# Last feed-forward stage with seven block products, and another order in the second block's mixers and first choice of experts

## What is computed

```
def swiglu(x, w_gu, w_down):                      # D_FF = 2816
    gate, up = jnp.split(x @ w_gu, 2, axis=-1)
    return (jax.nn.silu(gate) * up) @ w_down

def hybrid_layer(x, mem_n, ...):
    h = layer_norm(ALPHA * x + 0.5 * swiglu(x, ffn1...), ln_g[0], ln_b[0])
    ... merged = gated sum of the three branches ...
    h = layer_norm(ALPHA * h + merged @ w_out, ln_g[1], ln_b[1])
    return layer_norm(ALPHA * h + 0.5 * swiglu(h, ffn2...), ln_g[2], ln_b[2])

def second_block(x, mem, ...):
    for l in range(DEPTH):
        xn = rmsnorm(x, norm_mix[l]); proj = xn @ w_in[l]
        u_pool, u_conv, u_diff, u_sc, u_mem = jnp.split(proj, ...)
        cat = stack of pool_mixer, conformer_conv (31 taps), diff_attention, short_conv, memory_attention
        x = x + rmsnorm(cat, group_norm[l]) @ w_out[l]
        x = x + peer_ffn(rmsnorm(x, norm_ffn[l]), peer_wq[l], peer_subkeys[l], peer_u[l], peer_v[l])

def peer_ffn(xn, wq, subkeys, u_tab, v_tab):
    q = (xn @ wq).reshape(b, s, 8, 2, 128)
    top_s, top_i = lax.top_k(einsum(q, subkeys), 16)
    best, ci = lax.top_k(sums of the two halves' 16 x 16 scores, 16)
    idx = top_i[first, ci // 16] * 128 + top_i[second, ci % 16]
    g = softmax(best)
    out = sum over the 8 x 16 picks of g * gelu(u_tab[idx] . xn) * v_tab[idx]
```

## Time and profile before

| | us |
|---|---|
| median of 3 runs | 3241.88 (3241.27 to 3243.1) |
| the profiled execution | 3243.7 |
| its span | 3241.9 |
| TensorE busy in the span | 3016.5 (93%) |
| VectorE busy | 1940.5 (60%) |
| ScalarE busy | 644.6 (20%) |
| GpSimd busy | 615.3 (19%) |
| last feed-forward stage, gate-up from its second slab to the end of the way down | 1359 to 1581 |
| mixers and gathers, first layer | 1581 to 2414 |
| mixers and gathers, second layer | 2414 to 3235 |

### The profile page before, as it was taken

One profiled execution on the slowest core, in us unless ns is written; L12 is line 12 of the kernel. 1 busy time (PEld: TensorE's weight loads), 2 busy tenths in 40 slices (PEclk: granted clock), 3 DMA queues, 4 the chain that ended last, 5 costly groups with the idle time before them and its releaser, 6 DMA issues.

```text
span 3241.9 us, 34946 instructions
## 1 busy us (share of the span) xinstructions
PE 3016.5 (93%) x13098; PEld 2009.3 (62%) x13098; DVE 1940.5 (60%) x4473; ACT 644.6 (20%) x1581; POOL 615.3 (19%) x558
## 2 busy tenths in 40 slices
PE   8999999999999999999999888888989988888887
PEld 8958997995976898786685333333448643333322
DVE  7744432776764523210275877777757487777775
ACT  1113121111102223010153111111125321111110
POOL 0010000101001000100012434443421144444442
PEclk9999999999999999999999999999999999999999
DMA  6443223444543323464336999999983599999998
GB/s 232 174 157 128 104 92 129 178 174 156 195 171 141 130 79 115 145 248 154 112 116 237 422 421 418 417 412 414 420 357 119 202 421 421 421 412 416 416 417 351
DMA packets 114937, 830.38 MB, mean 256 GB/s; under 512 B 12880, under 2 KB 13136, under 8 KB 14160
## 3 DMA queue, kind: packets, MB, share of 16 engines
q0 software_dynamic: 73728, 536.90, 40.0%
q1 hardware_dynamic: 39456, 281.29, 24.1%
q10 hardware_dynamic: 1584, 9.95, 0.8%
HBM read 827.05 MB, written 1.05 MB: 255 GB/s over the span
## 4 chain that ended last, share of the span: by engine, by line
PE 65%; DMA 23%; DVE 6%; issue 4%; ACT 1%; POOL 0%; POOLq 0%; DVEq 0%; SPq 0%; ACTq 0%
DMA arena<-table_uv,idx 22%; PE bank L348 11%; PE bank L2444 9%; PE bank L443 9%; PE bank L503 6%; PE bank L701 5%; PE bank L375 4%; PE bank L430 4%; PE bank L937 3%; PE bank L2131 2%; PE bank L2316 2%; DVE arena L3025 1%; PE bank L599 1%; DVE diag L3033 1%; PE bank L2390 1%
## 5 line engine op out<-in xcount | busy, mean ns | idle before, releaser
L2444 PE MATMUL bank<-arena,diag 128*128 128x512 f32 x2048 | 1019.3, 624 | 187.7 <-DVE diag L3033 181.1
L2444 PEld LDWEIGHTS bank<-arena,diag 128*128 128x128 f32 x2048 | 361.5, 193 | 721.2 <-DVE diag L3033 453.3
L3025 DVE CUSTOM_DVE_ANT_0 arena<-arena 128x1024 f32<-128x1024 f32 x512 | 625.6, 1222 | 262.2 <-DMA arena<-table_uv,idx 258.9
L3109 POOL DMA_INDIRECT arena<-table_uv,idx x512 | 542.8, 1060 | 931.3 <-PE bank L2444 717.0
L2681 ACT ACTIVATE dots<-dots 128x1 f32<-128x1 f32 x512 | 103.8, 203 | 1089.9 <-DVE dots L3025 1089.6
L1811 POOL TENSOR_TENSOR x_tok<-arena,ktail 128x1024 f32<-128x1024 f32 (+1 forms) x12 | 27.0, 2251 | 1531.2 <-ACT arena L967 1531.2
L348 PE MATMUL bank<-x,ring 128*128 128x256 f32 x1440 | 316.0, 382 | 0.0
L348 PEld LDWEIGHTS bank<-x,ring 128*128 128x128 f32 x1440 | 275.5, 192 | 39.6 <-issue 1.9
L3033 DVE TENSOR_SCALAR diag<-cst,dots,soft 128x128 f32<-128x128 f32 x512 | 175.9, 344 | 0.0
L701 PE MATMUL bank<-x,ring 128*128 128x256 f32 x768 | 173.1, 379 | 0.0
L701 PEld LDWEIGHTS bank<-x,ring 128*128 128x128 f32 x768 | 143.2, 190 | 18.8 <-issue 1.0
(11 more groups left out here) (556 smaller groups left out, 4064.4 us busy)
## 6 DMA issues: line engine op xcount, KB each, us to landing
ring<-stream SPq DMA_DIRECT2D x258, 1024.0 KB, 4.8
arena<-table_uv,idx POOLq DMA_INDIRECT x512, 13.0
ktail<-ln_rows ACTq DMA_DIRECT2D x6, 1024.0 KB, 5.0
arena<-mem_rows SPq DMA_DIRECT2D x2, 1024.0 KB, 9.7
arena<-stream SPq DMA_DIRECT2D x2, 1024.0 KB, 6.9
sq<-keys ACTq DMA_DIRECT2D x2, 1024.0 KB, 4.7
cst<-consts SPq DMA_DIRECT2D x1, 1547.0 KB, 8.1
cst<-consts SPq DMA_DIRECT2D x1, 1089.0 KB, 14.4
```

The source lines that it names most:

```text
L2444: last = mm(bank[4 + 2 * tt + half][:, :], diag[:, n % DIAGS, :], row_slot(n)[:, D + 512 * half:D + 512 * half + 512], start=(h == 0 and k ...
L3025: v.tensor_tensor_reduce(u, u, tok[:, tt, :], 1.0, 0.0, ALU.mult, ALU.add, dots[:, tt, k:k + 1]).then_inc(u_used.sem, 1)
L3109: g.indirect_dma_start(out=row_slot(n), out_offset=None, in_=peer_uv, in_offset=bass.IndirectOffsetOnAxis(ap=idx[:, h % 2, tt, k:k + 1], a ...
```

## The change

The last feed-forward stage goes through `ffn_by_seven` too, and `ffn` is gone. Its sums have tiles of their own (`last_gu_space` of two sets instead of three, `last_down_space`, `last_x_space`, `last_h_space` with three sets, `last_r_space`, `last_p_space`), as the tiles of the other stages are overwritten by the second block's preparation. Hidden pairs are summed one at a time (`one_pair_sums`): pair 0 after slab 3, pair 1 after the last gate-up slab, the others ahead of the weight sums of the same slab on the way down. The norm is `norm_by_seven` with `last_rows` in place of the channel copies; before the second block TensorE waits for the first tile's scaling. SyncE loads memory rows and parameters with slabs 6 and 7 of the stage, and constants and the second block's first four slabs with slabs 25 to 29, ahead of the constants waiting for all hidden chunks. VectorE clears one tile a slab (slabs 5 to 9) and scales the memory rows at slab 11; the transposes of the memory go through two banks, one tile after slab 12 and one after slab 13.

In the mixers three roots of heads are taken as three Ln and three Exp; the copy of the pool projection stands after the fourth exponential; taps 8 to 10 of the convolution stand ahead of the difference and 11 to 20 behind it. The first choice of experts finds and writes eight numbers, then the other eight; gathers 0 to 7 need the first signal only, gather 8 the second.

```diff
+EARLY_AFTER = (6, 7) + tuple(range(GU_SLABS + 3, GU_SLABS + 8))
+EARLY_IN_GU = 2
...
+        last_gu_space = ((by_head(kT), by_head(qT)), (by_head(xaq), by_head(swq)))
+        last_down_space = ((by_tile(Q)[:, 0:HALF], by_tile(Q)[:, HALF:D], by_tile(qkT)[:, 0:HALF], flat_mem[:, 0:HALF]),
+                           tuple(arena[:, n * T:n * T + HALF] for n in (16, 18, 20, 22)),
+                           tuple(flat_x[:, n * HALF:n * HALF + HALF] for n in range(4)))
...
-                early = n - ((DEPTH - 1) * SLABS + FFN2_AT[DEPTH - 1] + 6)
-                if 0 <= early < EARLY_LOADS:
-                    if early == 0:
+                early = n - ((DEPTH - 1) * SLABS + FFN2_AT[DEPTH - 1])
+                if early in EARLY_AFTER:
+                    i = EARLY_AFTER.index(early)
+                    if i == 0:
                         sp.wait_ge(slab_done.sem, slab_done.at(DEPTH - 1, FFN2_AT[DEPTH - 1]))
-                    during_last(sp, early)
+                    if i == EARLY_IN_GU:
+                        sp.wait_ge(hid_ready.sem, hid_ready.at(DEPTH - 1, 2 * FC))
+                    during_last(sp, i)
...
-                to_channels(l, 2 * f, 0, y)
...
+                if last_stage(l, f):
+                    pe.wait_ge(z_dve.sem, z_dve.at(l, 2 * 2 + 1))
+                else:
+                    to_channels(l, 2 * f, 0, y)
...
+            def one_pair_sums(l, f, w):
+
+                dve.wait_ge(hid_ready.sem, hid_ready.at(l, f * FC + (2 if w == 0 else FC)))
+                if w >= 3:
+                    dve.wait_ge(slab_done.sem, slab_done.at(l, FFN2_AT[l] + GU_SLABS + w - 1))
+                a11, a12 = hidden[:, 2 * w, 0:P], hidden[:, 2 * w + 1, 0:P]
+                a21, a22 = hidden[:, 2 * w, P:T], hidden[:, 2 * w + 1, P:T]
+                s1, s2, s3, s4 = (hidden_sum((l, f), w, q) for q in range(1, 5))
+                step.did(v.tensor_tensor(s1, a21, a22, ALU.add))
+                step.did(v.tensor_tensor(s3, a11, a21, ALU.subtract))
+                dve.wait_ge(step.sem, step.n - 1)
+                step.did(v.tensor_tensor(s2, s1, a11, ALU.subtract))
+                step.join()
+                v.tensor_tensor(s4, a12, s2, ALU.subtract).then_inc(hs_ready.sem, 1)
...
-                    if j % 4 == 3 or j == GU_SLABS - 1:
+                    if last_stage(l, f):
+                        if j == 3:
+                            one_pair_sums(l, f, 0)
+                        during_last(dve, j)
+                    elif j % 4 == 3 or j == GU_SLABS - 1:
                         pair_sums(l, f, j // 4)
...
+                if last_stage(l, f):
+                    one_pair_sums(l, f, 1)
                 for i in range(GU_SLABS + 2, W_SLABS):
+                    if last_stage(l, f):
+                        one_pair_sums(l, f, i - GU_SLABS)
                     weight_sums(l, f, at, i)
...
-                by_channel(l, n, 0, x, gain, shift)
+                if final:
+                    last_rows(0)
+                else:
+                    by_channel(l, n, 0, x, gain, shift)
...
-                else:
-                    norm(l, 1, OUT_AT + OUT_SLABS)
-                    ffn(l, 1, FFN2_AT[l])
-                    norm(l, 2, SLABS)
+                norm(l, 1, OUT_AT + OUT_SLABS, lambda: weight_sums(l, 1, FFN2_AT[l], 0))
+                ffn_by_seven(l, 1, FFN2_AT[l])
+                norm_by_seven(l, 2, (lambda: weight_sums(l + 1, 0, FFN1_AT[l + 1], 0)) if l < DEPTH - 1 else None)
...
+            tt = j - MEM2_T_AT
+            if 0 <= tt < TT:
+                pe.wait_ge(mem_scaled, tt + 1)
+                if tt > 0:
+                    pe.wait_ge(mem_copied, 2 * tt)
...
+                def head_roots(*heads):
+                    for n, i, b in heads:
+                        act.wait_ge(qk_ms.sem, qk_ms.at(l, n + 1))
+                        step.did(fn(sq[:, 2 * i:2 * i + 2, :].rearrange("p c t -> p (c t)"), bank[b][:, :], ACT.Ln, bias=eps[:, 0:1]))
+                    step.join()
+                    for n, i, b in heads:
+                        root = sq[:, 2 * i:2 * i + 2, :].rearrange("p c t -> p (c t)")
+                        fn(root, root, ACT.Exp, scale=-0.5).then_inc(qk_std.sem, 1)
...
-                head_root(0, 1, 3)
-                head_root(1, 2, 4)
-                head_root(2, 0, 5)
+                head_roots((0, 1, 3), (1, 2, 4), (2, 0, 5))
...
+                    if n == POOL_COPY_AT:
+                        read(fn(pp[:, :, POOL_EDGE:POOL_EDGE + T], projected(S_POOL)[:, :].rearrange("p (a t) -> p a t", a=GT),
+                                ACT.Copy), S_POOL)
...
-                conv_part(8, 14)
+                conv_part(8, 11)
...
-                conv_part(14, 21)
+                conv_part(11, 21)
...
+                def first_choice():
+
+                    keys_first8(0, 0)
+                    keys_masked(0, 0)
+                    keys_next8(0, 0)
...
+                    step.did(v.max(best[:, 0, 0:8], sums))
+                    step.join()
+                    step.did(v.max_index(besti[:, 0:8], best[:, 0, 0:8], sums))
+                    places_of_half(0)
+                    step.did(v.match_replace(masked[:, :], best[:, 0, 0:8], sums, -3e38))
...
+                    v.max_index(besti[:, 8:16], best[:, 0, 8:16], masked[:, :]).then_inc(best_ready.sem, 1)
+                    dve.wait_ge(best_ready.sem, best_ready.at(l, 1))
+                    places_of_half(1)
...
-                for k in TOPK_PARTS:
-                    topk_part(0, 0, k)
+                first_choice()
...
-                        passed(idx_ready, idx_ready.at(l, h * TT + tt + 1))
+                        passed(idx_ready, idx_ready.at(l, 1 if n == 0 else h * TT + tt + 2))
+                    if n == TOPK // 2:
+                        passed(idx_ready, idx_ready.at(l, 2))
```

225 lines of the change are left out of this document (108 added, 117 removed).

## The result

The changed kernel takes 3222.91 us (median of 4 runs, 3222.45 to 3225.39); the kernel before, on the same chip, 3242.49. The ratio is 0.9938 with a 95% interval of [0.9926, 0.9949], so 16.5 to 24 us less. I had predicted 3219, range 3210 to 3228.

What follows compares the result with a forecast made beforehand. It took TensorE to bound the work from the last feed-forward stage into the second block, and DMA the gathers. Gains of 12.2 (stage), 9.6 (mixers) and 1.0 (first choice) sum to 22.8: 3241.9 to 3219 us, range 3210 to 3228.

Steps and rivals of the forecast that it cites:

- Steady part of the stage: Last feed-forward stage: 22 gate-up slabs take 133.3 us instead of 152, the last part 66.09 instead of 75.53.
- Entry: Start of the last feed-forward stage: VectorE's sums delay the x sums to about 1360.3; TensorE idles some 3.6 us.
- Handover: Last stage to second block: first tile ready 10.7 us after the last matmul; TensorE idles 3.8 us; transposes gain 15.2.
- rival (c): Clock doesn't fall at the two seams and gathers start 1.6 earlier at no price: 3212 to 3215, chance 0.13.
- two falls at 1.5 each: At the last stage's start and end, each new TensorE idle causes a clock fall costing 1.5 us, bounds 0 and 3.0.
- The stage's term, 12.2: Last feed-forward stage: net gain of 12.2 us, from 15.2 at the second block's transposes less 3.0 for clock falls.
- Mixers: Both layers' mixers: fewer table loads, earlier exponentials and moved taps gain 4.8 us a layer, 9.6 together.
- The eight steps beside GpSimd: Mixers: VectorE's steps to the difference overlap GpSimd's pool sums and lose 1.8 us, bounds no loss and 3.0.
- 3.0 from the Trainium skill: Mixers: upper bound of VectorE's loss before the difference, 3.0 us, if blocked by all GpSimd work left.
- One sign of being wrong: Mixers: a difference ready later than 16 us after the maxima would show the prediction wrong.
- First choice: First choice of experts: earlier gathers against a later second tile gain net 0.5 us a layer, bounds -0.5 and 1.6.
- the queue runs dry by 1.1 us: Gathers: ninth comes 1.2 us later, first eight end 1.6 earlier; with 1.7 us in hand the queue runs dry by 1.1.

Runs made afterwards that it cites:

- after_again: The changed kernel as it is, measured a second time beside the other runs: 3223.94 us, ratio 0.9943 to the kernel before.
- late_signal: The changed kernel, but GpSimd issues its first gather only when all sixteen numbers of the first choice are written: 3224.48 us.
- old_choice: The changed kernel with the first choice of experts and its signals as they were before: 3221.62 us.
- choice_fill: The changed kernel with 16 extra matmuls on TensorE where it stands still before the second tile's transposes: 3223.38 us.
- stage_alone: The kernel before with only the last feed-forward stage changed to seven products: 3230.59 us against 3243.6.
- mixers_alone: The kernel before with only the mixers changed (roots, pool copy, convolution taps): 3234.16 us against 3243.6.
- roots_alone: The kernel before with only three logarithms put before three exponentials for the head-square roots: 3239.63 us against 3243.6.
- choice_spread: The changed kernel, with the spread order: first eight numbers, second tile's sums, second eight maxima, their numbers during transposes; gate exponentials after the second tile's root: 3219.57 us.
- after: The changed kernel, all parts together, against the kernel before: 3222.91 us, ratio 0.9938.
- taps_back: The changed kernel with the convolution's taps split as before (8 to 13, then 14 to 20): 3226.79 us, ratio 0.9950 to the kernel before.

## Why the prediction was right, and where not

The measured 3222.9 is 4 us from the forecast of 3219. That it is not further off is partly luck, as two errors of opposite sign meet in the sum (end of this section).

- **Steady part of the stage**: right. From the x sums to the last part 135.9 us (forecast 136.0, with 0.61 of waiting at slab 12 for 0.9), the last part 66.1.
- **Entry**: right in its end in this profile, not in its parts. The x sums start at 1359.77 (forecast 1360.3), as the two slow weight sums cost the forecast 2.8 us each. TensorE's idle time is 1.99 for the third slab's fetch and 0.86, not 3.6 in one, and a fall of the clock between them (0.74 and 0.84 in the four us from 1352 and from 1356) fills the rest. VectorE ends this stretch, so the fall costs nothing: I had charged 1.5. How the four sums meet GpSimd's row operations differs between profiles: in four of the ten profiles with the new stage (after_again, late_signal, old_choice, choice_fill) only one of them was slow, and in the first three of these the x sums began 6.6 us after the start of VectorE's scaling instead of 8.7.
- **Handover**: right. TensorE waited 3.07 us (forecast 3.8), the clock fell to 0.57 for four us and the 16 value products took 1.2 us more there than for the second tile. But it doesn't fall each time: it did in five of the eight profiles that have this wait. In the profile of old_choice it stayed at 1.00 at both seams:

```profile
1350.00:1358.00 8.00, 5.92 (x49) 5.29 (x48) 7.33 (x14) 2.61 (x6) 5.84 (x2) 1.00 0.53 184
1566.00:1574.00 8.00, 4.94 (x27) 4.15 (x26) 5.75 (x11) 6.50 (x14) 2.98 (x2) 1.00 0.35 131
```

  That is rival (c) for the stage: the bet on two falls at 1.5 each was not safe. The stage's term, 12.2, measured 14.7 in the trace and 13.1 by stage_alone. Of the 2.5 more in the trace, 1.2 are the transposes' earlier start (16.4 ahead, not 15.2) and 1.3 the falls: 3.0 charged, 1.7 paid.
- **Mixers**: right, step by step. 9.6 forecast, 9.9 in the trace, 9.4 by mixers_alone. The wait before the scores is gone, the one at the difference 0.76 (forecast 0.8), the one at the convolution's mean 0.75 (1.0). The exponentials took 8.9 us with the copy (8.8), from their start to the difference 16.85 (16.8). By the Trainium skill (ScalarE: Activation LUTs, "Table sets: the hidden batching unit") Ln and Exp would have shared a table and 2.07 us a layer would have stayed. The trace shows a load of 1.28 us at each switch, and roots_alone the 4.0 us that went with them. The eight steps beside GpSimd cost 1.37 (4.62 against 3.25), for which the sum had 1.8. I had worked out 3.0 from the Trainium skill (SBUF — State Buffer, "Who interferes with whom"), by which two engines on the shared ports exclude each other for a whole instruction. In the four rows under **The taps** the trace agrees with that rule; what was wrong is my use of it, as if all that GpSimd had left stood in front of VectorE, while VectorE had begun first on one of the two long ones. One sign of being wrong was badly set: a difference later than 16 us after the maxima. It came 16.9 after them, and by my own times it would have come 16.9 after them too, so that sign tells nothing.
- **First choice: wrong, with the wrong sign by the bytes.** Forecast a gain of 0.5 a layer, bounds -0.5 and 1.6; by the bytes it is 1.5 behind at 60 us and 1.1 at 640, outside the bounds either way. The early start did come (7.87 against 10.06 us) and gained 1.0, as allowed. The ninth gather was forecast 1.2 later and came 2.6 and 1.9 later. What failed is the sentence that the queue runs dry by 1.1 us. I had let the ninth gather be late by VectorE's 1.2 alone. I had written myself that TensorE stands still in front of these transposes and that its clock falls there, and did not see that behind a longer standstill the fall is longer (about 3 or 7 us behind 2.95, about 7 or 10 behind 4.35). The second tile was 1.4 late, TensorE's first use 2.3 in the mean, and the eighth gather, which needs the second tile's queries to have left its slot, was 3.5 and 1.3 late (24.8 and 24.1 us after the score copy, before 21.3 and 22.8); I had left it out. So the loss by 60 us was 2.5, not 1.1.

In the trace the three add up to 14.7 + 9.9 - 4.2 = 20.4, against 12.2 + 9.6 + 1.0 = 22.8: the stage and the mixers gave 2.8 more than forecast, the choice 5.2 less (1.1 to 1.5 of its 2.1 a layer by the bytes, 1.4 by the means over five profiles each, the rest within the gathers' varying rate). So half of the choice's miss is hidden by what the other two gave in excess. The distance from 20.4 to the measured 19.6 lies within what these times can tell.

## What to carry to other kernels

An earlier signal is worth something only as long as the queue behind it can be refilled. Ask what frees the first slot, not only when the first transfer starts. If two consumers hang on one engine's list (here the gathers and the second tile), put in front what the slower of them needs, and lay the rest into that engine's waits: the spread order used 1.6 and 2.1 us of waiting and had moved more than both others at 60 us and at 640. And where an engine idles at a seam between two programs, look whether the other engines' order there is only the order in which they were written.

## What was unexpected in the hardware

- The falls of TensorE's clock behind one and the same wait differ between profiles. Behind the 3.07 us at the handover the clock fell to 0.50 in five of eight profiles (after, after_again, choice_spread, late_signal, taps_back) and stayed at 1.00 in three (old_choice, stage_alone, choice_fill). Behind the 2.95 us before the second tile it was low for about 3 or 7 us, never 0. My estimate from the stretches above (1.5 to 1.7 us at the handover, 1.1 to 1.3 a layer) is some 4 us at most between executions of one kernel.
- Where VectorE's four sums meet GpSimd's two row operations at the entry, two sums were slow in six profiles of the same code and one in four, and the x sums started up to 2.1 us apart.
- The gathers' rate over 100 us at a DMA share of 1.00 to 1.01 lay between 407 and 422 GB/s, and which stretch was the slow one differed between profiles: up to 2 us in 100 us. A difference of 2 us is better read from the bytes at its start than from the time behind such a phase.
- A signal of TensorE that came 2.1 and 2.0 us after the recorded end of its matmuls, in the two layers of choice_fill.
